# Three score units of the dilated attention ahead of the last row's value products, and the first layout by class one row sooner

## What is computed

```
hn = rms_norm(h, g_mix);  qd,kd,vd,qg,kg,vg = split(hn @ w_in)         # rotary on q and k
A: 4 heads of differential attention:
   a = softmax(q1 k1 / 8) - lam * softmax(q2 k2 / 8)
   o = rms_norm(a @ v, g_subln) * (1 - lam_init)                       # v is 128 wide
B: 8 heads of dilated window attention, each with the patterns (128,1), (512,4), (2048,16):
   o_p, lse_p = attention within radius 64 inside each class of tokens r mod dilation
   o = sum_p softmax(lse)_p * o_p
h = h + concat(A, B) @ w_out
h = h + relu(rms_norm(h) @ w_up)^2 @ w_down
h = h + sigmoid(rms_norm(h) @ w_gate) * (p @ w_ple);  out = rms_norm(h)
```

## Time and profile before

| | |
|---|---|
| median of 3 runs | 3125.66 us (3122.2 to 3128.05) |
| the profiled execution | 3128.39 us, its span 3125.8 us |
| mean granted TensorE clock | 0.997 |
| busy: PE, DVE, ACT, POOL | 98%, 61%, 51%, 42% of the span |
| passage from differential to dilated attention | about 1141 to 1160 us from the span's start |
| head 0 of the dilated phase, first unit to first unit of head 1 | 1145.10 to 1184.33 us |

### The profile page before, as it was taken

How to read it: one execution, slowest core, us unless ns; L and a number is a source line. 1 busy time by engine, 2 the same in 40 slices (tenths; PEclk the granted TensorE clock), 3 DMA queues, 4 the chain that set the end, 5 groups by cost and what they waited for, 6 DMA issues and landing times. The chain is left out here.

```text
span 3125.8 us, 48238 instructions
## 1 busy us (share of the span) xinstructions
PE 3069.6 (98%) x17024; PEld 2646.9 (85%) x17024; DVE 1903.6 (61%) x3225; ACT 1582.0 (51%) x2863; POOL 1311.0 (42%) x1094
## 2 busy tenths in 40 slices
PE   8999999999999999999999999999999999999998
PEld 8888889888889889998887888788878888888787
DVE  6134333898999966666556754776545444445876
ACT  5011111687888878885235555555543333333544
POOL 2023332011111146672235666666676665664233
PEclk9999999999999999999999999999999999999999
DMA  5234335403040338765764776478596668666322
GB/s 184 90 105 130 113 117 162 112 23 88 22 88 23 90 77 201 183 143 171 257 204 142 256 231 197 148 252 263 202 286 196 197 225 274 196 196 215 126 86 72
DMA packets 466301, 495.49 MB, mean 159 GB/s; under 512 B 83856, under 2 KB 370960, under 8 KB 460816
## 3 DMA queue, kind: packets, MB, share of 16 engines
q1 hardware_dynamic: 462720, 486.12, 50.8%
q10 hardware_dynamic: 3344, 6.29, 0.8%
HBM read 324.15 MB, written 168.17 MB: 157 GB/s over the span
## 5 line engine op out<-in xcount | busy, mean ns | idle before, releaser
L2451 POOL TENSOR_TENSOR h_u_lo<-h_u_raw,h_u_hi 128x512 fp32r<-128x512 f32 x222 | 370.9, 1697 | 211.4 <-ACT h_u_hi L2447 211.4
L136 PE MATMUL h_acc<-h_w_hi,h_u_hi 128*128 128x512 f32 x896 | 349.4, 390 | 2.4 <-POOL h_u_lo L2451 2.4
L138 PE MATMUL h_acc<-h_w_hi,h_u_lo 128*128 128x512 f32 x896 | 349.3, 390 | 0.0
L137 PE MATMUL h_acc<-h_w_lo,h_u_hi 128*128 128x512 f32 x896 | 349.2, 390 | 0.0
L810 DVE TENSOR_REDUCE c_neg_half<-c_scores 128x1 f32<-128x1024 f32 x256 | 312.6, 1221 | 42.2 <-PE c_scores L897 42.1
L2540 DVE TENSOR_TENSOR h_h<-h_acc,h_h 128x512 f32<-128x512 f32 x224 | 153.2, 689 | 281.7 <-PE h_acc L138 281.6
L767 ACT ACTIVATE c_piece<-c_scores,c_neg_max 128x1024 f32<-128x1024 f32 x256 | 286.7, 1120 | 58.9 <-DMA s_vd<-a_hl 35.6
L920 PE MATMUL c_pv<-c_v,c_piece 128*128 128x128 f32 x2048 | 270.3, 275 | 0.4 <-ACT c_o L781 0.4
L920 PEld LDWEIGHTS c_pv<-c_v,c_piece 128*128 128x128 f32 x2048 | 248.6, 192 | 0.7 <-ACT c_o L781 0.5
L2447 ACT CAST h_u_hi<-h_u_raw 128x512 fp32r<-128x512 f32 x224 | 127.9, 619 | 228.2 <-DMA h_u_raw<-s_u 228.1
L732 POOL TENSOR_SCALAR c_mean<-c_ssq,c_eps 128x1 f32<-128x1 f32 x64 | 18.8, 293 | 505.1 <-ACT c_o_junk L788 475.4
(11 more groups left out here) (237 smaller groups left out, 7992.5 us busy)
## 6 DMA issues: line engine op xcount, KB each, us to landing
h_u_raw<-s_u SPq DMA_DIRECT2D x224, 256.0 KB, 3.5
s_u<-e_u SPq DMA_DIRECT2D x192, 256.0 KB, 3.7
s_qkt<-a_hl SPq DMA_DIRECT2D x128, 256.0 KB, 2.8
e_a<-w_up_dram SPq DMA_DIRECT2D x64, 512.0 KB, 4.4
h_w_raw<-s_t SPq DMA_DIRECT2D x32, 1024.0 KB, 7.9
h_w_raw<-w_down_dram SPq DMA_DIRECT2D x24, 1024.0 KB, 7.8
b_kt<-s_qkt SPq DMA_DIRECT2D x64, 256.0 KB, 8.9
e_t<-w_down_dram SPq DMA_DIRECT2D x32, 512.0 KB, 5.4
```

The source lines that it names most:

```text
L136: nc.tensor.matmul(out, lhs_hi, rhs_hi, start=first, stop=False, skip_group_check=onto)
L137: nc.tensor.matmul(out, lhs_hi, rhs_lo, start=False, stop=False, skip_group_check=onto)
L138: return nc.tensor.matmul(out, lhs_lo, rhs_hi, start=False, stop=last, skip_group_check=onto)
L2451: op(self.u_lo[q][s][:], self.u_raw[q][s][:], self.u_hi[q][s][:].bitcast(F32), ALU.subtract).then_inc(self.S["u_lo"], 1)
```

## The change

Five edits, which belong together:

- **PE.** `values` of row 63 leaves the differential loop and becomes `differ.last_values`, called in the dilated loop after `score(2)` (`w == TURN - 1`). PE's order is then `score(0), score(1), score(2), values(63, 0..3), turn(0), score(3), ...`.
- **ACT.** `o_copy(63)` and `square(63)` move behind `exp(1)` and ahead of `e_copy(0)` (`w == TURN`).
- **POOL.** `pool_rest` ends with row 62. Then comes `spread(0, 1)`, then the root of row 63, then the wait for all value products, the two memsets and `spread(0, 2)`.
- **DVE.** `result(63)` moves behind `mask(15)` and ahead of `output(11)` (`w == 2 * PAIRS`).
- **SP.** Its program text does not change.

```diff
 (scalar, differential loop)
-                        if q == 0 and n >= 2:
-                            o_copy(n - 2)
+                        if q == 0 and 2 <= n <= STEPS:
+                            o_copy(act, n - 2)
...
-                        if q == 1 and n >= 2:
-                            square(n - 2)
+                        if q == 1 and 2 <= n <= STEPS:
+                            square(act, n - 2)
 (vector, differential loop)
-                        if q == 3 and n >= 2:
-                            result(n - 2)
+                        if q == 3 and 2 <= n <= STEPS:
+                            result(dve, n - 2)
 (tensor, differential loop)
-                        if 0 <= n - 1 < STEPS:
-                            values(n - 1, q)
+                        if 0 <= n - 1 < STEPS - 1:
+                            values(pe, n - 1, q)
 (what the phase hands on)
         def pool_rest(pool):
-            for n in range(SPLIT, STEPS):
+            for n in range(SPLIT, STEPS - 1):
                 root(pool, n)
+        def last_root(pool):
+            root(pool, STEPS - 1)
+        def last_values(pe):
+            for g in range(4):
+                values(pe, STEPS - 1, g)
+        def last_square(act):
+            o_copy(act, STEPS - 1)
+            square(act, STEPS - 1)
+        def last_result(dve):
+            result(dve, STEPS - 1)
 (dilated phase: scalar, vector, gpsimd, tensor)
+                    if w == TURN:
+                        differ.last_square(act)
                     if TURN <= w < TOTAL + TURN:
                         e_copy(w - TURN)
...
+                    if w == 2 * PAIRS:
+                        differ.last_result(dve)
                     if OUT <= w < TOTAL + OUT - 1:
                         output(dve, w - OUT)
...
                 differ.pool_rest(pool)
+                spread(0, 1)
+                differ.last_root(pool)
                 differ.wait_values(pool)
                 zero(10, kt[1][:, :, :EDGE])
                 zero(11, kt[1][:, :, EDGE + SEQ:])
-                spread(0, 1)
                 spread(0, 2)
...
                     if w < TOTAL:
                         score(w)
+                    if w == TURN - 1:
+                        differ.last_values(pe)
```

More of the change, by code:

```diff
@@ L627, in project_phase @@
                      wait_constants, TAIL, last_values, last_out, wait_bank)
-Differed = namedtuple("Differed", "sync_step sync_rest pool_rest wait_head2 wait_values wait_results wait_stored")
+Differed = namedtuple("Differed", "sync_step sync_rest pool_rest wait_head2 wait_values wait_results wait_stored last_root "
+                      "last_values last_square last_result")
 def differential_phase(kit, block, fixed, project):
@@ L737, in root, with o_copy, square, result @@
             nc.gpsimd.tensor_tensor(rstd[:, s:s + 1], mean[:], half[:], ALU.pow).then_inc(S["rstd"], 1)
+        def o_copy(act, n):
+            act.wait_ge(S["pv"], 4 * n + 4)
+            if n >= 2:
+                act.wait_ge(S["out"], n - 1)
+            nc.scalar.copy(o[:, n % 2], pv[:, :VD]).then_inc(S["o"], 1)
+        def square(act, n):
+            act.wait_ge(S["o"], n + 1)
+            act.wait_ge(S["ssq"], n)
+            if n >= 2:
+                act.wait_ge(S["mean"], n - 1)
+            nc.scalar.activation(o_junk[:], o[:, n % 2], ACT.Square,
+                                 accum_out=ssq[:, n % 2:n % 2 + 1]).then_inc(S["ssq"], 1)
+        def result(dve, n):
+            s = n % 2
+            dve.wait_ge(S["rstd"], n + 1)
+            if n >= 2:
+                dve.wait_ge(stored[s], n // 2 * 16)
+            nc.vector.scalar_tensor_tensor(out=out[:, s], in0=o[:, s], scalar=rstd[:, s:s + 1],
+                                           in1=gain[:], op0=ALU.mult, op1=ALU.mult).then_inc(S["out"], 1)
+        def values(pe, n, g):
+            h, s = n // TILES, n % 2
+            if g == 0:
+                pe.wait_ge(S["o"], n)
+                if n == 0:
+                    project.wait_bank(pe, 1)
+                pe.wait_ge(v_in[h % 2], 16 * (h // 2 + 1))
+            pe.wait_ge(S["at"], 4 * n + g + 1)
+            for c in range(4 * g, 4 * g + 4):
+                ins = nc.tensor.matmul(pv[:, :VD], at[s][c // 8][:, c % 8 * P:c % 8 * P + P], v[h % 2][:, c], start=(c == 0), stop=(c == KT - 1))
+            ins.then_inc(S["pv"], 1)
         if True:
@@ L775, in a_copy @@
                     nc.scalar.copy(at[n % 2][g // 2][:, g % 2 * 512:g % 2 * 512 + 512], turned[:]).then_inc(S["at"], 1)
[L777 to L789, removed]
                 for n in range(-2, STEPS + 2):
@@ L844, in combine @@
                                                    in1=e[s][0][f][:], op0=ALU.mult, op1=ALU.add).then_inc(S["a"], 1)
[L846 to L852, removed]
                 project.wait_constants(dve)
@@ L909, in turn @@
                     ins.then_inc(S["a_turned"], 1)
[L911 to L921, removed]
                 for n in range(-2, STEPS + 1):
@@ L956, in wait_stored @@
                 sp.wait_ge(stored[s], 16 * STEPS // 2)
-    return Differed(sync_step, sync_rest, pool_rest, wait_head2, wait_values, wait_results, wait_stored)
+    return Differed(sync_step, sync_rest, pool_rest, wait_head2, wait_values, wait_results, wait_stored, last_root,
+                    last_values, last_square, last_result)
 Dilated = namedtuple("Dilated", "last_values last_output wait_stored wait_banks wait_results wait_pattern1")
```

## The result

The changed kernel takes 3133.91 us (median of 12 runs, 3131.46 to 3137.36), the kernel before, run on the same chips, 3125.59 us (12 runs). The ratio is 1.0026, 95% interval 1.0018 to 1.0033: 8 us slower, where 3.3 were forecast. It lies outside the range given, 3121.5 to 3133. The profiled execution of the changed kernel took 3132.9 us with a span of 3130.8.

The account below looks back on a forecast made before the run. PE, busy 98% of the span, was taken as the bound, with about 4 us idle at the passage. Late loads +6.3, gain -4.5, clock +1.5 summed to +3.3 on 3125.66, so 3129.0 us; range 3121.5 to 3133.

Parts of the forecast that it names:

- the one on DVE: DVE at the passage into head 0: `mask(0)` follows `result(62)` and starts at 1143.25, 4.20 us sooner.
- g: Gain of PE at the passage, up to the score of unit 8: 4.5 us.
- the sum: Whole kernel: 6.3 lost to late loads, minus 4.5 gained, plus 1.5 for the clock, +3.3 us.
- the one on DMA rings: Rule weighed for SP's loads: ring descriptors go in order, completion may not; shared engines would make the sum about +14.
- The queue: SP: head 1's loads wait behind row 63's store, go out 21.5 us later, and idle PE 6.3 us before unit 24.
- 6.3 - g: Change of the time from late loads before unit 24: a loss of 6.3 us less the passage's gain.
- The clock: PE after the hole before unit 24: one stretch at half clock, costing 1.5 us, bounds 0 and 3.
- The layout: POOL's `spread(0, 1)`: starts after row 62's root, lasts 11.74 us, ends level with PE at unit 8, 1154.8.
- The second layout: POOL's `spread(0, 2)`: ends at 1168.1 at the latest, unit 16 wants it at 1168.9, 0.8 us of cover, no cost.
- head 2's loads and the stores behind them: SP's queue behind head 1's loads: first output store, `load_qk(2)`, next stores; claimed to cost nothing.
- transfers share the queue: Rival, 5%: head 2's loads and the store slow head 1's loads, up to +14; half of it gives 3133.
- the passage doesn't gain: Rival, 14%: POOL's layout starts or finishes late, g goes to 0, the loads' loss stays: +7.8, 3133.5.

Follow-up runs that it names:

- e7: The changed kernel with `result(63)` behind `mask(8)` instead of `mask(15)`, nothing else: 3125.58 us, ratio 1.0000 to the kernel before.
- e2: The changed kernel, but POOL waits for `result(62)` before the first layout, the loads staying late: 3130.86 us, ratio 1.0013 to the kernel before.
- e3: The changed kernel with head 1's loads issued ahead of row 63's store and POOL waiting for `result(62)`: 3123.47 us, ratio 0.9986 to the kernel before.
- e4: The changed kernel with the first cast of POOL's first layout split into four pieces, nothing else: 3132.51 us, ratio 1.0015 to the kernel before.
- e1: The changed kernel, but SP issues head 1's loads ahead of the store of row 63: 3125.28 us, ratio 0.9993 to the kernel before.
- e8: The kernel before with only `result(63)` moved behind `mask(15)`: 3137.32 us, ratio 1.0037 to the kernel before.
- e5: The changed kernel with `result(62)` beside `result(63)` behind `mask(15)`, and head 1's loads ahead of both rows' stores: 3122.28 us, ratio 0.9988 to the kernel before.

## Why the prediction was wrong

**The step that failed** is the one on DVE: "`result(62)` still stands ahead of the masks and starts at 1142.98, for the same root as before; `mask(0)` follows it as it now follows `result(63)`, 0.27 later". It started on time and lasted 3.95, because the same change puts a POOL cast beside it. So `turn(0)` came 0.6 sooner instead of 2.80, which takes 2.2 from g: 4.5 becomes 2.3, and e7, whose clock did not fall there, has 2.2. The hole that should have gone stayed at 2.46, and in this execution a stretch at 1.2 GHz behind it took 1.5 more: g was 0.7. The prediction had put the clock at the passage at nothing, since the hole was to vanish. e2, e3 and e4 show the cause: without a cast beside it 0.35, with a quarter of one 1.19. With the hold known, `mask(0)` comes at 1142.98 + 3.9, near 1146.9 instead of 1147.45, and the sum is 6.3 - 2.3 + 1.5 = +5.5; with a second stretch at the low clock, at the passage, it is +7.0. Most of what is left of the 7.8 is 0.4 in the loads and 0.2 in the clock behind them. The Trainium skill has the rule (SBUF — State Buffer, SBUF: two separate sides, and its summary of rules): the port pair that VectorE and GpSimd share is an exclusive lock, which whoever starts first holds for its whole instruction, and a VectorE operation with two SBUF inputs needs it against a GpSimd operation that reads SBUF. The trace agrees: 3.95 for the operation with two SBUF inputs, 0.41 for the one with a single SBUF input and one in PSUM, and 1.19 where the cast is cut. That it is the second SBUF input, and not the kind of instruction, no run here shows by itself. This is the rule that should have been weighed, and the one on DMA rings that was weighed changed nothing.

**The queue** was right as a mechanism and in size. Loads 0.75 behind `result(63)`, 17.1 us to the last landing for 16.7, a hole of 6.56 for 6.3; 6.3 - g with the measured g is 5.6, and the 0.4 of slower loads makes 6.0, where the table has 6.1. e1 removes this loss alone, e8 makes it alone.

**The clock** behind the new hole was 1.7 (units 24 to 32: 13.53 instead of 11.83) for 1.5.

**The layout** on POOL was right: 11.7 us from the root of row 62. It ends nearly level with PE where neither engine is held: in e5 0.23 of hole is left and unit 8 is the 4.5 sooner of the forecast. The second layout had its cover, no hole at unit 16. That head 2's loads and the stores behind them cost no hole on PE was right too. The rival "transfers share the queue" was hardly put to the test: the issue of head 2's first load, begun at 1177.67, lasted 10.73 us, to 0.2 before the last landing, so that its 3.1 MB never stood beside the loads of head 1, only a store of 512 KB and at most that one load. With these behind them the loads of head 1 took 17.1 us in the changed kernel, 17.0 in e2 and 17.4 in e4, without them 16.7 before and 16.6 in e1: at most 0.8 for that rival.

**The rival** "the passage doesn't gain", 14% at 3133.5, is the case that came, in place and price; but its reason was another, and the price met in part by luck: it let POOL be late. The hold alone leaves g at 2.3, outside that rival; only the second fall of the clock, which follows such a hole in some executions, brings it to 0.7. POOL was on time, and DVE waited for it without a semaphore. The argument against it, that the masks run beside this layout today, was true and about the wrong instruction. What was missing is to ask, of every instruction that has a new neighbour after the move, what it reads and what the neighbour reads.

## What to carry to other kernels

An instruction moved on one engine changes what stands beside instructions of the others that were not moved: where GpSimd (POOL) gets work of several microseconds on SBUF tiles, list VectorE's (DVE's) operations on two SBUF tiles in that stretch, and keep them out (e5), split GpSimd's work (e4), or let it wait (e2, e3). When an operation is deferred because its result "is not needed", look for what stands behind its reader in a queue: here a 64 KB store that no engine needed soon made 3 MB of loads 25 us later, counted from the reference point (8.3 before, 33.4 after). Write the cover of each such queue down before spending it (20 us here, and e7, which spends 12.6, loses nothing).

## What was not expected of the hardware

- A DVE instruction with two SBUF inputs beside a POOL cast lasted as long as the rest of that cast: 3.95, 1.19 and 1.61 us for 0.35, with the rest of the cast 3.8, 1.0 and 1.5.
- A hole on PE of about 2.46 us was followed by 1.2 GHz in some profiled executions (the changed kernel, e1) and not in others (e7, and the kernel before with 2.45), and such a stretch at the passage cost 1.5 us. In e8 one of 2.98 ended in 6.8 us of it.
- SP's issue of the first load of head 2 took 10.73 us in the changed kernel, with twelve loads and a store ahead of it in the queue, where such an issue takes 0.4. No hole on PE followed from it here; why SP waited there is open.
